# Scores of the 64-wide attention heads issued in pairs, in different row halves of the array

## The reference, cut to what matters

```
hn = rms_norm(x, attn_norm)
qa, ka, va, cq, ckv, kr, gates = split(hn @ w_in)
qa, ka = rope(rms_norm(heads(qa))), rope(rms_norm(heads(ka)))   # 8 heads x 64
sc = einsum('qd,kd->qk', qa, ka) / sqrt(64);  sc = where(kpos <= qpos, sc, -1e30)
ya = softmax(sc) @ va                                           # A, per head
... the same for B from cq, ckv, kr, 8 heads x 96 ...
merged = sigmoid(g_a) * (ya @ w_br_a) + sigmoid(g_b) * (yb @ w_br_b)
x = x + merged @ w_out
x = x + ffn(rms_norm(x))
```

## Time and profile before

| | us |
|---|---|
| median of 3 runs | 1391.2 (1389.51 to 1394.19) |
| the profiled execution | 1390.43 |
| its span | 1388.6 |
| busy in the span: PE, weight loads, DVE, ACT | 1341.9, 1174.6, 1043.4, 889.5 |
| mean granted TensorE clock | 0.991 |

### The profile page before, as it was taken

How to read it: one execution, slowest core, us unless ns; L and a number is a source line. 1 busy time by engine, 2 the same in 40 slices (tenths; PEclk the granted TensorE clock), 3 DMA queues, 4 the chain that set the end, 5 groups by cost and what they waited for, 6 DMA issues and landing times.

```text
span 1388.6 us, 19242 instructions
## 1 busy us (share of the span) xinstructions
PE 1341.9 (97%) x7166; PEld 1174.6 (85%) x7166; DVE 1043.4 (75%) x957; ACT 889.5 (64%) x932; POOL 82.9 (6%) x67
## 2 busy tenths in 40 slices
PE   6999989999989999889999999999999999999996
PEld 6889978888978899777888888988888889889885
DVE  5786566544457775767889898898898898988984
ACT  6575535443446755546777687777776877877773
POOL 0220000000003200000000000000000010000000
PEclk9999999999999999989999999999999999999999
DMA  7633345665546434498999999999999999999991
GB/s 252 221 92 122 122 152 189 207 189 166 176 154 209 128 92 134 157 390 290 317 379 380 375 391 380 370 373 389 373 382 376 376 381 381 373 389 372 381 354 48
DMA packets 180525, 381.29 MB, mean 275 GB/s; under 512 B 8650, under 2 KB 63476, under 8 KB 180468
## 3 DMA queue, kind: packets, MB, share of 16 engines
q1 hardware_dynamic: 175248, 369.12, 74.6%
q0 software_dynamic: 2304, 8.39, 2.3%
q10 hardware_dynamic: 2916, 3.01, 0.7%
HBM read 374.20 MB, written 6.29 MB: 274 GB/s over the span
## 4 chain that ended last, share of the span: by engine, by line
PE 89%; DVE 4%; ACT 4%; issue 2%; DMA 1%; ACTq 0%; SPq 0%; POOLq 0%; DVEq 0%
PE ps L1017 17%; PE ps L1019 17%; PE ps L1018 17%; PE ps L628 8%; PE ps L630 7%; PE ps L629 7%; PE ps L635 2%; PE ps L636 2%; PE ps L637 2%; ACT w_hi L1172 2%; PE ps L1070 1%; DVE w_lo L1510 1%; PE ps L744 1%; PE ps L751 1%; DVE mix L1688 1%
## 5 line engine op out<-in xcount | busy, mean ns | idle before, releaser
L1748 DVE TENSOR_TENSOR w_lo<-mix,w_hi 128x2048 fp32r<-128x2048 f32 (+2 forms) x192 | 394.7, 2068 | 81.4 <-ACT w_hi L1379 80.3
L1379 ACT CAST w_hi<-mix 128x2048 fp32r<-128x2048 f32 (+2 forms) x190 | 329.3, 1737 | 129.5 <-PE ps L1019 129.5
L1017 PE MATMUL ps<-w_hi,eT_hi 128*128 128x512 f32 (+1 forms) x768 | 289.8, 377 | 1.1 <-DVE eT_lo L1895 1.1
L1018 PE MATMUL ps<-w_lo,eT_hi 128*128 128x512 f32 (+1 forms) x768 | 285.7, 372 | 0.0
L1019 PE MATMUL ps<-w_hi,eT_lo 128*128 128x512 f32 (+1 forms) x768 | 285.7, 372 | 0.0
L1510 DVE TENSOR_TENSOR w_lo<-raw,w_hi 128x2048 fp32r<-128x2048 f32 (+4 forms) x94 | 198.7, 2119 | 114.3 <-ACT w_hi L1172 113.4
L1172 ACT CAST w_hi<-raw 128x2048 fp32r<-128x2048 f32 (+4 forms) x94 | 166.6, 1777 | 123.2 <-PE ps L630 106.5
L1748 DVE TENSOR_TENSOR w_lo<-raw,w_hi 128x2048 fp32r<-128x2048 f32 (+1 forms) x96 | 209.7, 2201 | 17.5 <-ACT w_hi L1379 16.9
L1379 ACT CAST w_hi<-raw 128x2048 fp32r<-128x2048 f32 (+1 forms) x96 | 175.3, 1842 | 40.6 <-PE ps L1019 37.7
L1017 PEld LDWEIGHTS ps<-w_hi,eT_hi 128*128 128x128 f32 x768 | 144.7, 188 | 20.3 <-DVE eT_lo L1895 1.1
L1019 PEld LDWEIGHTS ps<-w_hi,eT_lo 128*128 128x128 f32 x768 | 144.5, 188 | 20.4
(11 more groups left out here) (194 smaller groups left out, 1948.5 us busy)
## 6 DMA issues: line engine op xcount, KB each, us to landing
mix<-in_expert_w_gate_up_dram SPq DMA_DIRECT2D x79, 1024.0 KB, 7.9
raw<-in_expert_w_gate_up_dram SPq DMA_DIRECT2D x49, 1024.0 KB, 7.8
mix<-in_expert_w_down_dram SPq DMA_DIRECT2D x49, 1024.0 KB, 8.9
mix<-in_expert_w_gate_up_dram SPq DMA_DIRECT2D x48, 768.0 KB, 9.0
raw<-in_expert_w_down_dram SPq DMA_DIRECT2D x31, 1024.0 KB, 8.8
raw<-in_w_in_dram SPq DMA_DIRECT2D x28, 1024.0 KB, 5.4
raw<-in_dense_w_gate_up_dram SPq DMA_DIRECT2D x16, 1024.0 KB, 5.2
raw<-in_expert_w_gate_up_dram SPq DMA_DIRECT2D x16, 768.0 KB, 8.1
```

The source lines that it names most:

```text
L1017: pe.matmul(out_, l_hi, w_hi[q][:, cols], start=first, stop=False, skip_group_check=True)
L1018: pe.matmul(out_, l_hi, w_lo[q][:, cols], start=False, stop=False, skip_group_check=True)
L1379: act.copy(w_hi[q][:, 0:m], e_raw[raw_of(p, first)][:, 0:m]).then_inc(e_hi_ready, 1)
L1748: dve.tensor_tensor(w_lo[q][:, 0:m], e_raw[raw_][:, 0:m], w_hi[q][:, 0:m].bitcast(F32), ALU.subtract).then_inc(e_split, 1)
```

## The change

`scores` takes a tuple of heads: it first makes all waits, then issues the first product of each head, then the second of each. A new function says which heads are issued at step k: at even k two heads of A, at odd k none, as long as k + 2 is below 8; B's heads stay one at a time. The planner follows the same order, so the banks in turn change: heads 0 to 7 now have banks 1, 2, 3, 0, 3, 0, 3, 0, and the turned probabilities 0 to 5 have 1, 2, 1, 2, 1, 3. From k = 6 on, banks and order are those of before.

```diff
+def scores_at(k):
+
+    n = k + AHEAD
+    if n < HEADS:
+        return (n, n + 1) if n % 2 == 0 else ()
+    return (n,) if n < 2 * HEADS else ()
...
         for k in range(16):
-            if k + AHEAD < 16:
-                tile["s", l, k + AHEAD] = banks.turns(4)
+            for n in scores_at(k):
+                tile["s", l, n] = banks.turns(4)
             tile["pT", l, k] = banks.turns(4)
...
-                def scores(k):
-
-                    evacuated(tile["aT", l, k // 2] if k < HEADS else tile["bT", l, k - HEADS])
-                    t_ = tile["s", l, k]
-                    start(t_)
-                    q, key = q_k(k)
-                    pe.matmul(ps[t_.bank][:, 0:P], q[:, 0:P], key[:, 0:P], start=True, stop=True)
-                    pe.matmul(ps[t_.bank][:, P:3 * P], q[:, P:T], key, start=True, stop=True).then_inc(filled[t_.bank], 1)
+                def scores(heads):
+
+                    for k in heads:
+                        evacuated(tile["aT", l, k // 2] if k < HEADS else tile["bT", l, k - HEADS])
+                        start(tile["s", l, k])
+                    for k in heads:
+                        q, key = q_k(k)
+                        pe.matmul(ps[tile["s", l, k].bank][:, 0:P], q[:, 0:P], key[:, 0:P], start=True, stop=True)
+                    for k in heads:
+                        t_ = tile["s", l, k]
+                        q, key = q_k(k)
+                        pe.matmul(ps[t_.bank][:, P:3 * P], q[:, P:T], key, start=True, stop=True).then_inc(filled[t_.bank], 1)
...
-                for k in range(AHEAD):
-                    scores(k)
+                scores(range(AHEAD))
                 kv_up(1)
                 for k in range(16):
-                    if k + AHEAD < 16:
-                        scores(k + AHEAD)
+                    scores(scores_at(k))
                     turn_probs(k)
```

## The result

| | before | after |
|---|---|---|
| median of 22 runs, us | 1390.34 | 1392.69 |
| ratio, 95% interval | | 1.0018 (1.0012 to 1.0024) |
| profiled span, us | 1388.6 | 1390.3 |
| PE busy, us | 1341.9 | 1338.1 |

The forecast was 1392.9 with a range of 1388.0 to 1396.0. Six heads' scores came off PE's path and the kernel became 2.35 us slower. The loss is too small for the bound of 0.3% set in the prediction, but with 22 runs a side it is clear of noise.

What follows compares the result with a forecast made beforehand. PE was taken to bound the kernel, busy 97% of the span. Pair gains less stalls (+0.16 us) and one clock fall (+1.50) made 1391.2 + 1.66 = 1392.9 us, range 1388.0 to 1396.0.

Steps and rivals of the forecast that it cites:

- the bound of 0.3%: Smallest difference a measurement of this kernel can tell from no change: 4.2 us, so bounds of 1387.0 and 1395.4.
- What bounds the kernel: In the attention loop PE is busy 67.90 of 68.09 us, so PE time removed or stalls added both count.
- 0.94 us for a lone odd head, 0.01 for one in a pair: PE cost of an odd head's scores; three leaving the path give 2.82 us a layer, 5.6 in all, if nothing waits.
- The order rule: Products start and end strictly in program order; the sum would then be about 1391.9.
- The stall: At k = 2 in both layers PE waits 2.73 us for DVE's evacuation of head 3; net +0.16 us over both layers.
- No stall at k = 4: The pair of heads 6 and 7 finds head 5's bank free, by a margin of 0.13 us.
- The clock: PE's clock may fall behind each k = 2 stall: chance one in two, 1.50 us each; one fall taken, +1.50.
- the forecast without the clock: Loop from the scores at k = 0 to those at k = 6: 30.20 us.
- a sign that the prediction had set: In the profile after, k = 6's scores stand at about 111.6 us as before.
- The full gain: Rival: DVE evacuates head 3 before PE arrives, so all 5.6 us stay, 1385.6 us; chance 0.08.
- Halves that do not overlap: Rival: a pair costs another 0.85 us, 3.6 in all, 1394.8, or 1396.3 with one clock fall; chance 0.07.

Runs made afterwards that it cites:

- the wait alone: Kernel before, without pairs, plus one wait: ahead of head 4's scores (k = 2) PE waits for head 3's evacuation; 1397.95 us, ratio 1.0046.
- moved pieces: Changed kernel with the three pieces of B's norm that DVE does between heads 2 and 3 moved behind head 3; 1392.70 us, ratio 1.0014.
- other banks: Changed kernel with banks written out for k below 8, so that no pair waits for the odd head two before; 1388.90 us, ratio 0.9989.
- run on order: Changed kernel with the pair's products issued head by head, both of the even head first, waits and banks unchanged; 1392.92 us, ratio 1.0015.
- one row half: Changed kernel with mixer A's odd heads computing their even neighbour's scores, so both heads use partitions 0 to 63; 1399.29 us, ratio 1.0051.
- the two small waits taken out: Kernel with other banks, plus values ahead of a B head's transposes and ACT's cast for gate pair 5 one step later; 1383.07 us, ratio 0.9939.
- the two edits without pairs: Kernel before with its own banks, plus values ahead of B heads' transposes and ACT's gate pair 5 cast one step later; 1389.82 us, ratio 0.9994.
- scores behind the gates for k below 8: Changed kernel, banks in turn, scores behind gates only for k below 8, plus values before B transposes and later gate pair 5 cast; 1383.56 us, ratio 0.9948.

## Why the prediction was right, point by point

- **What bounds the kernel** held: a wait put into the loop showed in the time (the wait alone, 7.2 us more), and so did PE time taken out of it once nothing waited (7.7 us less).
- **0.94 us for a lone odd head, 0.01 for one in a pair** held: 0.86 us a pair and 0.22 us between values and transposes at k = 3 were measured. That 0.65 of it is side-by-side work is shown by the run with both heads in one half (1.51 us). The 0.94 is slightly low: from the scores of k = 4 to those of k = 6, at the full clock, it is 113.62 - 104.20 = 9.42 us for 111.53 - 101.12 = 10.41, so 0.99, since the transposes' first row is 0.50 behind values and 0.55 behind a 64-row head.
- **The order rule** of the Trainium skill ("TensorE: Matmul & The Clock Gate", Part 3), that products start and end in program order, fell as a forecast: head-by-head order gave the same pair, 0.86 us.
- **The stall** was forecast at 2.73 us at k = 2 in both layers and measured at 2.75 in both; the pair stood 12.12 us behind k = 0's, for a forecast of 12.03. The small difference is the release, which took 92.76 - 92.61 = 0.15 us and not 0.06. That DVE's program sets it, and not when the scores were issued, is shown by moving the pieces.
- **No stall at k = 4** held, but the margin of 0.13 us was not put to the test, since the low clock behind k = 2 made PE late there; the run with moved pieces shows that the wait is real.
- **The clock** was the term that was mis-sized. I gave each stall one chance in two and a price of 1.50 us. It fell at both, and at all ten such stalls of five kernels, so one in two was too low; the loops came out 2.78 and 1.51 us above the forecast without the clock. For the same reason the scores of k = 6 stood at 113.62 and not at about 111.6, a sign that the prediction had set.
- **That the number came so close is in part luck.** The loops lost 4.45 us in the profile, where the forecast had 1.66 in all. The profile after had two falls fewer and one more elsewhere, which gave back 1.66 us, and began the loop 0.77 earlier, none of it forecast. The forecast of 1392.9 also started from a median of three runs, 1391.2; over 22 runs the kernel before has 1390.34. What the medians owe to falls elsewhere, for a difference of 2.35, is not known, since one execution of each kernel was profiled.
- **The full gain** as a rival fell, for the reason given against it, that nothing makes DVE earlier. It would have failed without the stall as well: even with the wait out of the way (other banks) each loop gained only some 1.15 of its 2.82 us, since DVE's norm and a weight's DMA held the rest. The prediction took the stall as the only thing between 1392.9 and 1385.6; it was the first of three waits.
- **Halves that do not overlap** fell. Its price of 0.85 us a pair was too high as well: 0.65 was measured with both heads in one half.

## What to carry to other kernels

Two heads issued at once need two free banks at once: before pairing work on one engine, list who empties each bank that the pair takes, and what stands ahead of that in the emptying engine's program. A wait in a tight PE loop can cost more than its length: here stalls of 1.9 to 2.75 us brought 1.5 to 2.8 us of lower clock on top. So hide it behind products that need nothing of it, and then check the same bank order to the end of the loop. When a stall is taken out, read the profile for the next, since the gain comes in full only behind the last of them.

## What the runs showed of the hardware that was not expected

- Two products in different row halves start out of the order that kernel.py gives them: with both products of the even head ahead of those of the odd head, all four records of both first products start before the first of the even head's second (81.06 and 81.38 us in the run on order; 0.86 us for two heads, 0.85 for one). The trace gives the line of each record, not its place in the compiled program, so whether the engine or the compiler changes the order was not shown.
- Five kernels had a stall of 1.88 to 2.75 us in a loop that had run at the full clock (the change, and the runs on order, on one row half, on moved pieces and on the wait alone), two stalls each. In their profiles the clock fell at the end of all ten or just behind. The kernels without such a stall (before, other banks, the two small waits taken out, the two edits without pairs, scores behind the gates for k below 8) kept the full clock through the loop in both layers. Idle stretches of 1.90, 2.14 and 3.29 us elsewhere were followed by a fall in some executions and not in others, as in the two profiles shown here. What makes the difference was not tested.
